# The second half of the row gather and the row scales, moved behind the first down piece

## The chip, the core and the metric

The kernel runs on one core of a Trainium2 chip. The metric is the device time of one execution in microseconds (us); lower is better. Everything is float32 at the inputs and outputs.

## What is computed

A decoder block of 256 tokens with a width of 1024: a token mixer (gated recurrences), a cross-attention, and a mixture of experts, each added to the residual, and a last RMSNorm. The part in question is the mixture:

```
logits = h @ w_router + b_router              # 256 x 32
top_v, top_i = top_k(logits, 4);  gates = softmax(top_v)
for each expert e, for the tokens that chose it:
    gu   = x_rows @ w_gate_up[e] + b_gate_up[e]        # 1024 -> 2048
    gate = min(gu[:, :1024], 7);  up = clip(gu[:, 1024:], -7, 7)
    act  = (up + 1) * gate * sigmoid(1.702 * gate)
    y[tokens] += gates * (act @ w_down[e] + b_down[e]) # 1024 -> 1024
```

There are 32 experts. Each has 8 MiB of gate-and-up weights and 4 MiB of down weights in float32, and about 32 of the 1024 assignments.

## The kernel before, in words

Everything is written out by hand: each engine has one list of instructions in a fixed order, and semaphores are the only thing between the lists.

**Blocks.** Each expert's rows are handled in blocks of 64 (`ROWS`). With the given inputs every expert has one block, so there are 32 blocks; the profile shows it as 32 activations. Expert 0 is the `lead` (it is written out with some extra work), experts 5 to 28 run in a loop of three experts (`LOOPED`), expert 31 is `final` and has an order of its own.

**The weight ring.** The weights go through a ring of 11 slots of 2 MiB (`RING`, `SLOT`). An expert has six pieces: four of gate-and-up (k = 0 to 3) and two of down (k = 4, 5). Experts 0 to 3 and 29 to 31 are loaded piece by piece (L475; L487 for the last expert's down pieces), experts 4 to 28 in pairs of 4 MiB (`load_wide`, L459). All of these transfers are issued by SyncE, in the order of the experts, and each waits until TensorE has used what lay in its slots: `chunk_used` goes up by one at the end of each piece. A pair waits for the use of what lay in the second of its two slots. For instance: the first pair of expert 4 waits for piece (2, 3), its second pair for (2, 5), that is the second down piece of expert 2; its third for (3, 1). Piece (2, 3) waits for (0, 4), the first down piece of expert 0; (3, 3) for (1, 4). Pieces (3, 4), (3, 5) wait for (2, 0), (2, 1).

**One block on TensorE** (`expert`), for an expert that isn't the last:

1. gate-and-up: four pieces, two row tiles each, into `bank_g` and `bank_u` (`pair_of_inner`, L1090; 64 f32 matmul records of 512 columns, two halves of the array side by side). The weights of a piece are waited for (`chunk_in`).
2. `scatter_and_combine`: the rows of the block before are added to the output banks (L1113), and the gate selection is turned over into `bank_d` (L1192).
3. `next_rows(0)`: the first half of the gather for the next block, 24 bf16 matmuls into `bank_a` (L1128). A gather picks the rows of the next block from three bf16 parts of the tokens with the 0/1 matrix `sel`.
4. `flip_act` twice: the activations are turned over, half into `bank_u`, half into `bank_g` (L1201, 4 matmuls). ScalarE copies each half into `actT` (signals `actT_ready` and `actT_rest`).
5. `next_rows(1)`: the second half of the gather, 24 matmuls; then `scales` (L1104, 4 matmuls), which puts the row scales of the next block into `bank_g`, once `actT_rest` says that the bank is free. Its signal is `xb_psum`.
6. down: two pieces, four row tiles each (`pair`, L1081; 16 records per piece). They wait for `comb_ready` and `actT_ready`, and from the third row tile on for `actT_rest`. Each piece signals `chunk_used`.
7. the bias of the next block into `bank_g` and `bank_u` (L1090 again, 4 bf16 matmuls), after `one_hot_ready` and `xb_ready`.

VectorE waits for `xb_psum`, copies the scales (L2262), multiplies the gathered rows by them (L2096, signal `xb_ready`), then makes the selections for the block after the next one (L2072, L2078). ScalarE's activations and copies all have the line of one helper, L1315.

In the last expert the order differs: the two gather halves stand behind the first and second gate-and-up piece, down follows the flip directly, and the scales come after down.

The functions that the change touches:

Of the kernel before, what the change touches and what calls it, by code (L numbers as in the profile page):

```python
# [143 lines left out]
def build(nc, A, out):  # L144

    ctx = ExitStack()
    with ctx:
# [5 lines left out]
        sem = {n: ctx.enter_context(nc.semaphore(n)) for n in SEMS}  # L153
# [14 lines left out]
        def part(slot, first, last):  # L168
            return ring[:, slot * SLOT + first:slot * SLOT + last]
# [465 lines left out]
        def _(pe):  # L635
# [465 lines left out]
            def scales():  # L1101

                for t in range(NT):
                    last = pe.matmul(bank_g[:, 0:ROWS], all_ones, scaled_sel[:, t, :], start=(t == 0), stop=(t == NT - 1))  # L1104
                return last
# [17 lines left out]
            def gather(tiles):  # L1123

                for k in tiles:
                    for i in range(3):
                        for t in range(NT):
                            last = pe.matmul(bank_a[:, k * ROWS:(k + 1) * ROWS], h2_parts[:, i, t, rows_of(k)], sel[:, t, :],  # L1128
                                             start=(i == 0 and t == 0), stop=(i == 2 and t == NT - 1), skip_group_check=True)
                return last  # L1130
# [44 lines left out]
            def expert(e, slots, counts, last_tile=None, lead=False, final=False):  # L1175

                def next_rows(half):
                    pe.wait_ge(sem["sel_ready"], pe.snap(w1 + 1))
                    gather(range(half * KT // 2, (half + 1) * KT // 2))

                def scatter_and_combine():

                    pe.wait_ge(sem["yb_ready"], w1)
                    if lead:
                        pe.wait_ge(sem["down_bias_in"], 32)
                        pe.wait_ge(sem["seeded"], 2 * NT)
                        pe.wait_ge(sem["gT_ready"], 1)
                    scatter()

                    pe.wait_ge(sem["selg_ready"], w1)  # L1190
                    for t in range(NT):
                        last = pe.matmul(bank_d[:, t * P:(t + 1) * P], selg[:, t, :], ident[:, :], start=True, stop=True,  # L1192
                                         is_transpose=True, skip_group_check=True)
                    last.then_inc(sem["comb_psum"], 1)

                def flip_act(bk, half, by_quarter):

                    n = DOWN_ROWS // 2
                    for i in range(n):
                        src = act_t[:, half * QUARTER + i:(half + 1) * QUARTER:n] if by_quarter else act_t[:, half * n + i::DOWN_ROWS]  # L1200
                        last = pe.matmul(bk[:, i * P:(i + 1) * P], src, ident[:, :], start=True, stop=True, is_transpose=True,  # L1201
                                         skip_group_check=True)
                    return last

                if lead:
                    blocks = pe.alloc_register("blocks_of_lead")
                    pe.reg_mov(blocks, 1)
                else:
                    blocks = pe.value_load(table[0:1, bass.ds(e, 1)], min_val=1, max_val=MAXB)
                    first = pe.value_load(table[0:1, bass.ds(e + E, 1)], min_val=0, max_val=MAXW)  # L1210
                with pe.Fori(0, blocks) as c:
                    w1 = pe.snap(c + 1 if lead else first + c + 1)

                    pe.wait_ge(sem["xb_ready"], w1)
                    for k in range(GU_CHUNKS):
                        wk = part(slots[k], 0, SLOT)
                        if counts[k] is not None:
                            pe.wait_ge(chunk_in[slots[k]], counts[k])
                        tiles_of = [(a, bk) for a in range(GU_TILES) for bk in range(2)]
                        if k == GU_CHUNKS - 1 and not final:  # L1220
                            tiles_of = [(a, bk) for bk in range(2) for a in range(GU_TILES)]
                        for a, bk in tiles_of:
                            f = k * GU_TILES + a
                            if lead and (f, bk) == (KT // 2, 0):
                                pe.wait_ge(sem["xb_rest"], 1)
                            if last_tile is not None and (f, bk) == (KT - 1, 0):
                                pe.wait_ge(last_tile, 16)
                            c = a * 2 * D + bk * D
                            last = pair_of_inner((bank_g, bank_u)[bk], xbT[:, f, :], wk[:, c:c + D], False, f == KT - 1)
                            if (f, bk) == (KT - 1, 0):  # L1230
                                last.then_inc(sem["gate_done"], 1)
                            if lead and (f, bk) == (0, 1):
                                last.then_inc(sem["lead_half"], 1)
                        last.then_inc(sem["chunk_used"], 1)
                        if final and k < 2:
                            next_rows(k)
                        if lead and k == 1:
                            pe.wait_ge(sem["table_ready"], 1)
                            pe.reg_load(blocks, table[0:1, 0:1])
                            pe.wait_ge(sem["gates_ready"], 1)  # L1240
                            pe.wait_ge(sem["yb_ready"], w1)
                            one_time()

                    scatter_and_combine()
                    if not final:
                        next_rows(0)

                    pe.wait_ge(sem["act_ready"], w1)
                    if not final:
                        pe.wait_ge(sem["act_rest"], w1)  # L1250
                    flip_act(bank_u, 0, final).then_inc(sem["actT_psum"], 1)
                    if final:
                        pe.wait_ge(sem["act_rest"], w1)
                    flip_act(bank_g, 1, final).then_inc(sem["actT_rest_psum"], 1)

                    if not final:
                        next_rows(1)
                        pe.wait_ge(sem["actT_rest"], w1)
                        pe.wait_ge(sem["scaled_ready"], pe.snap(w1 + 1))
                        scales().then_inc(sem["xb_psum"], 1)  # L1260

                    pe.wait_ge(sem["comb_ready"], w1)
                    pe.wait_ge(sem["actT_ready"], w1)
                    for j in range(DOWN_CHUNKS):
                        wk = part(slots[GU_CHUNKS + j], 0, SLOT)
                        if counts[GU_CHUNKS + j] is not None:
                            pe.wait_ge(chunk_in[slots[GU_CHUNKS + j]], counts[GU_CHUNKS + j])
                        for a in range(DOWN_ROWS):
                            f = DOWN_ROWS * j + a
                            if final:  # L1270
                                h, i = divmod(a, DOWN_ROWS // 2)
                                f = DOWN_ROWS * h + DOWN_ROWS // 2 * j + i
                                if (j, a) == (DOWN_CHUNKS - 1, DOWN_ROWS // 2):
                                    pe.wait_ge(last_half_in, 32)
                                if (j, a) == (DOWN_CHUNKS - 1, 0):
                                    pe.wait_ge(sem["actT_rest"], w1)
                            elif (j, a) == (0, DOWN_ROWS // 2):
                                pe.wait_ge(sem["actT_rest"], w1)
                            last = pair(bank_d, actT[:, f, :], wk[:, a * D:(a + 1) * D], (j, a) == (0, 0),
                                        (j, a) == (DOWN_CHUNKS - 1, DOWN_ROWS - 1))  # L1280
                        last.then_inc(sem["chunk_used"], 1)
                    if final:
                        pe.wait_ge(sem["scaled_ready"], pe.snap(w1 + 1))
                        scales().then_inc(sem["xb_psum"], 1)

                    pe.wait_ge(sem["one_hot_ready"], pe.snap(w1 + 1))
                    pe.wait_ge(sem["xb_ready"], pe.snap(w1 + 1))
                    bias_of(bank_g, 0)
                    bias_of(bank_u, D)
# [1027 lines left out]
```

## Time and profile before

| | |
|---|---|
| median of 3 runs | 1203.46 us (1202.25 to 1204.08) |
| profiled execution | 1201.65 us, its span 1199.9 us |
| mean granted clock of TensorE | 0.986 |
| busy: TensorE | 1149.7 us (96%) |
| busy: VectorE | 378.3 us (32%) |
| busy: ScalarE | 169.7 us (14%) |
| DMA, mean over the span | 371 GB/s |
| read from HBM | 443.20 MB |

The span is the time from the first to the last instruction of the profiled execution. The busy share is an average over stages with different limits; the slices and windows below show them apart. The mixture of experts runs from about 290 us to the end. A matmul's duration in the records includes what it overlaps with its neighbours, so costs on TensorE are better read from the start of one group to the start of the next. `PEld` is the weight load of TensorE, `SPq` the issue of a transfer by SyncE.

### The profile page before, as it was taken

How to read it: one execution, taken by the hardware profiler on the slowest of the kernel's cores; microseconds unless marked ns; L12 is line 12 of the kernel's file. 1: busy time of each engine (PE TensorE's matmuls, PEld its weight loads, DVE VectorE, ACT ScalarE, POOL GpSimd, SP SyncE). 2: the span in 40 equal slices, each digit the busy share in tenths (PEclk: the TensorE clock that was granted, in tenths of full speed). 3: DMA queues.
4: the chain of work that ended last, by engine and by line, in shares of the span. 5: the costliest groups of instructions: out<-in, count | busy, mean ns of one | idle time of the engine just before them, and what ended most of it. 6: DMA issues, size and time to landing. Idle time of an engine off the chain costs nothing.

```text
span 1199.9 us, 17776 instructions
## 1 busy us (share of the span) xinstructions
PE 1149.7 (96%) x7104; PEld 577.8 (48%) x7105; DVE 378.3 (32%) x889; ACT 169.7 (14%) x340; POOL 18.3 (2%) x57
## 2 busy tenths in 40 slices
PE   9999999999999999999999999999999999999996
PEld 5989869956434434333334343333333333333332
DVE  4788777646222221112212121211111111111113
ACT  4311421253100000000001000000000000000002
POOL 2000010000000000000000000000000000000000
PEclk9999999999999999999999999999999999999998
DMA  8953200997999999999999999999999999999995
GB/s 282 387 192 116 107 9 22 399 347 295 413 427 417 430 434 429 430 434 430 433 430 435 429 431 435 428 433 431 435 429 431 433 430 432 434 433 424 424 427 210
DMA packets 41554, 444.85 MB, mean 371 GB/s; under 512 B 6164, under 2 KB 6628, under 8 KB 25640
## 3 DMA queue, kind: packets, MB, share of 16 engines
q1 hardware_dynamic: 40616, 441.62, 88.0%
q0 software_dynamic: 480, 1.85, 0.6%
q10 hardware_dynamic: 416, 0.79, 0.2%
q8 instruction: 29, 0.48, 0.2%
q14 instruction: 13, 0.11, 0.0%
HBM read 443.20 MB, written 1.05 MB: 370 GB/s over the span
## 4 chain that ended last, share of the span: by engine, by line
PE 68%; DMA 31%; ACT 0%; DVE 0%; SPq 0%; issue 0%; DVEq 0%; ACTq 0%
DMA ring<-in_w_gate_up 30%; PE bank L1090 22%; PE bank L1081 13%; PE bank L714 6%; PE bank L710 4%; PE bank L1113 4%; PE bank L1128 3%; PE bank L693 2%; PE bank L702 2%; PE bank L758 2%; PE bank L796 1%; PE bank L1020 1%; PE bank L1201 1%; PE bank L1104 1%; PE bank L1192 1%; PE bank L933 1%
## 5 line engine op out<-in xcount | busy, mean ns | idle before, releaser
L1090 PE MATMUL bank<-ring,region 128*64 128x512 f32 x2048 | 463.8, 608 | 37.5 <-DMA ring<-in_w_gate_up 37.5
L1090 PEld LDWEIGHTS bank<-ring,region 128*64 128x64 f32 x2048 | 147.4, 140 | 335.5 <-issue 270.4
L1081 PE MATMUL bank<-ring,region 128*64 128x512 f32 x1024 | 227.0, 595 | 0.5 <-DMA ring<-in_w_down 0.3
L2116 DVE TENSOR_SCALAR region<-bank 128x512 f32<-128x512 f32 x32 | 22.1, 691 | 575.2 <-PE bank L1090 575.2
L1081 PEld LDWEIGHTS bank<-ring,region 128*64 128x64 f32 x1024 | 71.0, 137 | 130.5 <-issue 126.7
L1315 ACT ACTIVATE region<-bank 128x256 f32<-128x256 f32 (+1 forms) x134 | 55.5, 440 | 372.7 <-PE bank L1081 251.5
L1315 ACT ACTIVATE bank<-region 128x512 f32<-128x512 f32 x32 | 19.2, 602 | 453.8 <-DVE region L2116 453.8
L714 PE MATMUL bank<-ring 128*128 128x256 f32 x336 | 73.8, 380 | 0.0
L714 PEld LDWEIGHTS bank<-ring 128*128 128x128 f32 x336 | 63.3, 190 | 9.3 <-issue 0.5
L1113 PE MATMUL bank<-region 64*128 64x512 f32 x264 | 65.6, 615 | 0.0
L1128 PEld LDWEIGHTS bank<-region,r_levels 128*128 128x128 bf16 x1584 | 63.1, 117 | 1.8 <-issue 1.6
L1128 PE MATMUL bank<-region,r_levels 128*128 128x64 bf16 x1584 | 63.3, 197 | 0.0
L710 PE MATMUL bank<-ring 128*128 128x128 f32 x448 | 50.7, 275 | 0.0
L710 PEld LDWEIGHTS bank<-ring 128*128 128x128 f32 x448 | 50.3, 192 | 0.3 <-issue 0.2
L1113 PEld LDWEIGHTS bank<-region 64*128 64x128 f32 x264 | 22.7, 186 | 41.9 <-issue 41.5
L1315 ACT ACTIVATE ring<-bank 128x256 f32<-128x256 f32 (+4 forms) x64 | 26.3, 433 | 116.6 <-PE bank L714 45.4
L2119 DVE TENSOR_SCALAR region<-bank 128x512 f32<-128x512 f32 x32 | 22.1, 691 | 32.0 <-PE bank L1090 32.0
L2262 DVE COPY stat<-bank 128x64 f32<-128x64 f32 x31 | 7.0, 225 | 58.5 <-PE bank L1104 58.5
L2072 DVE TENSOR_SCALAR region<-region 128x64 bf16 (+1 forms) x64 | 13.3, 251 | 37.8 <-issue 37.8
L1201 PE MATMUL bank<-ident,region 128*128 128x128 f32 x128 | 23.2, 304 | 0.0
L2123 DVE SCALAR_TENSOR_TENSOR region<-region 128x512 f32<-128x512 f32 x32 | 22.2, 692 | 3.3
L2096 DVE TENSOR_TENSOR region<-bank,stat 128x512 f32<-128x512 f32 (+1 forms) x33 | 22.3, 674 | 1.7 <-PE bank L1128 0.6
(279 smaller groups left out, 783.1 us busy)
## 6 DMA issues: line engine op xcount, KB each, us to landing
ring<-in_w_gate_up SPq DMA_DIRECT2D x50, 4096.0 KB, 29.8
ring<-in_w_down SPq DMA_DIRECT2D x25, 4096.0 KB, 34.4
ring<-in_w_gate_up SPq DMA_DIRECT2D x24, 2048.0 KB, 16.6
ring<-in_w_down SPq DMA_DIRECT2D x11, 2048.0 KB, 11.7
ring<-in_w_in SPq DMA_DIRECT2D x6, 2048.0 KB, 17.8
ring<-in_w_xkv SPq DMA_DIRECT2D x4, 2048.0 KB, 10.2
ring<-in_w_gate_up SPq DMA_DIRECT2D x7, 1024.0 KB, 35.2
ring<-in_w_out SPq DMA_DIRECT2D x2, 2048.0 KB, 8.0
```

What stands on the lines that cost most here:

```text
L693: last = pe.matmul(bk[:, i * T:(i + 1) * T], w[:, k, (m + i) * P:(m + i + 1) * P], rhs[:, k, :], start=(k == 0), stop=(k == KT - 1))
L702: last = pe.matmul(bk[:, :], lhs[:, k, t * P:(t + 1) * P], w[:, k, :], start=(k == 0), stop=(k == KT - 1))
L710: last = pe.matmul(bk[:, i * P:(i + 1) * P], right[:, k, i * P:(i + 1) * P], left[:, k, :], start=(first and i == 0 and k == 0), stop=(k = ...
L714: last = pe.matmul(bk[:, 0:T], left[:, k, :], right[:, k, :], start=(first and k == 0), stop=(k == 3), skip_group_check=True)
L758: last = pe.matmul(bk[p:p + m, c * m:(c + 1) * m], rows[:, j * P + p:j * P + p + m], rows[:, i * P + p + shift:i * P + p + shift + m], sta ...
L1081: last = pe.matmul(bk[half * ROWS:(half + 1) * ROWS, :], lhs, w[:, half * 512:(half + 1) * 512], start=start, stop=stop, skip_group_check= ...
L1090: last = pe.matmul(rows, lhs, columns[:, half], start=start, stop=stop, skip_group_check=True)
L1113: last = pe.matmul(bank_y[t][half][:, :], combT[rows, t * P:(t + 1) * P], yb[rows, :], start=False, stop=False, skip_group_check=True)
L1128: last = pe.matmul(bank_a[:, k * ROWS:(k + 1) * ROWS], h2_parts[:, i, t, rows_of(k)], sel[:, t, :], start=(i == 0 and t == 0), stop=(i == ...
L1201: last = pe.matmul(bk[:, i * P:(i + 1) * P], src, ident[:, :], start=True, stop=True, is_transpose=True, skip_group_check=True)
L1315: return nc.scalar.activation(out_, in_, func, **kw)
L2096: v.tensor_tensor(xbT[:, lo:hi, :], src, row_scales.unsqueeze(1).broadcast_to([P, hi - lo, ROWS]), ALU.mult).then_inc(signal, 1)
```

## The change

The block of `next_rows(1)`, the wait for `scaled_ready` and `scales()` is taken from between the flip and the down stage, and put behind the first of the two down pieces. Its wait for `actT_rest` is dropped; the down loop has the same wait ahead of the third row tile of the first piece, so it has been passed by then. The last expert isn't changed.

```diff
@@ -1253,12 +1253,6 @@
                         pe.wait_ge(sem["act_rest"], w1)
                     flip_act(bank_g, 1, final).then_inc(sem["actT_rest_psum"], 1)
 
-                    if not final:
-                        next_rows(1)
-                        pe.wait_ge(sem["actT_rest"], w1)
-                        pe.wait_ge(sem["scaled_ready"], pe.snap(w1 + 1))
-                        scales().then_inc(sem["xb_psum"], 1)
-
                     pe.wait_ge(sem["comb_ready"], w1)
                     pe.wait_ge(sem["actT_ready"], w1)
                     for j in range(DOWN_CHUNKS):
@@ -1279,6 +1273,10 @@
                             last = pair(bank_d, actT[:, f, :], wk[:, a * D:(a + 1) * D], (j, a) == (0, 0),
                                         (j, a) == (DOWN_CHUNKS - 1, DOWN_ROWS - 1))
                         last.then_inc(sem["chunk_used"], 1)
+                        if j == 0 and not final:
+                            next_rows(1)
+                            pe.wait_ge(sem["scaled_ready"], pe.snap(w1 + 1))
+                            scales().then_inc(sem["xb_psum"], 1)
                     if final:
                         pe.wait_ge(sem["scaled_ready"], pe.snap(w1 + 1))
                         scales().then_inc(sem["xb_psum"], 1)
```

## Rows read from the trace of the kernel before

**Rows 1.** The page, part 2: GB/s of the DMA in 40 equal slices.
```profile
GB/s 282 387 192 116 107 9 22 399 347 295 413 427 417 430 434 429 430 434 430 433 430 435 429 431 435 428 433 431 435 429 431 433 430 432 434 433 424 424 427 210
```
**Rows 2.** Windows by stage: us, busy of each engine, granted clock, DMA share, GB/s.
```profile
370.00:376.00 6.00, 6.00 (x32) 2.10 (x30) 0.00 (x0) 0.60 (x1) 0.00 (x0) 1.00 0.96 374
...
450.00:550.00 100.00, 100.00 (x646) 41.15 (x644) 20.38 (x52) 8.98 (x20) 0.00 (x0) 1.00 1.00 430
600.00:700.00 100.00, 93.62 (x592) 37.54 (x591) 18.27 (x50) 8.21 (x19) 0.00 (x0) 0.97 1.00 432
```
**Rows 3.** Waits of TensorE over the span: us in total, times, longest.
```profile
PE bank L1090 <- DMA ring<-in_w_gate_up: 37.5, 23, 2.6
```
**Rows 4.** Chain of waits, 330 to 375: start, us, what; down of experts 1 and 2.
```profile
339.33 7.02 PE bank L1081 x32
...
365.45 7.02 PE bank L1081 x32
```
**Rows 5.** Timeline at 1170 to 1178: start, us, engine, line, tiles, idle before.
```profile
1175.47 0.39 PEld L1090 LDWEIGHTS bank<-ring,region 128*64 128x64 f32 x4 [0.47 <-DMA ring<-in_w_gate_up]
```
**Rows 6.** Timeline at 362 to 373: the turn of expert 2.
```profile
363.45 0.73 PE L1201 MATMUL bank<-ident,region 128*128 128x128 f32 x4
...
363.97 0.66 ACT L1315 ACTIVATE region<-bank 128x256 f32<-128x256 f32 x2 [0.74 <-PE bank L1201]
364.02 0.96 PE L1128 MATMUL bank<-region,r_levels 128*128 128x64 bf16 x24
...
364.81 0.64 PE L1104 MATMUL bank<-scaled_sel,region 128*128 128x64 f32 x4
...
365.38 7.09 PE L1081 MATMUL bank<-ring,region 128*64 128x512 f32 x32
...
365.75 0.69 DVE L2096 TENSOR_TENSOR region<-bank,stat 128x512 f32<-128x512 f32 x1
365.86 0.14 PEld L1081 LDWEIGHTS bank<-ring,region 128*64 128x64 f32 x2 [0.28 <-issue]
...
372.30 0.62 PE L1090 MATMUL bank<-region 128*64 128x512 bf16 x4
...
372.51 0.33 SPq L459 DMA_DIRECT2D ring<-in_w_gate_up  x1
```
**Rows 7.** Timeline at 1126 to 1200: expert 30's down, the last expert's gather and down.
```profile
1156.11 3.65 PE L1081 MATMUL bank<-ring,region 128*64 128x512 f32 x16 [0.27 <-DMA ring<-in_w_down]
1159.59 0.62 PE L1090 MATMUL bank<-region 128*64 128x512 bf16 x4
...
1160.83 3.65 PE L1090 MATMUL bank<-ring,region 128*64 128x512 f32 x16 [0.61 <-DMA ring<-in_w_gate_up]
1164.41 0.88 PEld L1128 LDWEIGHTS bank<-region,r_levels 128*128 128x128 bf16 x24 [0.81 <-issue]
...
1179.73 0.76 PE L1201 MATMUL bank<-ident,region 128*128 128x128 f32 x4
...
1180.68 7.09 PE L1081 MATMUL bank<-ring,region 128*64 128x512 f32 x32 [0.20 <-ACT region L1315]
```
**Rows 8.** Transfers issued around 245, 316, 360 and at 372.5 (landing alone), by line.
```profile
L475 SPq DMA_DIRECT2D ring<-in_w_gate_up x2: 327/385/443, 245.5 to 245.9; - x2
...
DMA to landing us min/median/max: 8.0/9.6/11.2
...
L475 SPq DMA_DIRECT2D ring<-in_w_gate_up x1: 340/340/340, 316.8 to 316.8; - x1
...
DMA to landing us min/median/max: 9.2/9.2/9.2
...
L459 SPq DMA_DIRECT2D ring<-in_w_gate_up x1: 328/328/328, 360.6 to 360.6; - x1
...
DMA to landing us min/median/max: 14.4/14.4/14.4
...
DMA to landing us min/median/max: 12.4/12.4/12.4
```

## The prediction

> **What bounds the kernel now.** I read the page first: busy shares, then the DMA line of the 40 slices. TensorE is busy 96% of the span, and from the eleventh slice on, up to the last, the DMA moves 413 to 435 GB/s [rows 1]. Both look full, so the page alone can't say which one ends the time. The windows by stage can [rows 2]: TensorE is busy 100 of 100 us at 450 to 550, but 93.6 at 600 to 700, while the DMA share is 1.00 in both, at 430 and 432 GB/s. The waits say the same: TensorE waited 37.5 us in all, 23 times, and for gate-and-up weights [rows 3].
>
> The reason is in two prices. An expert's weights are six pieces of 2 MiB, 12.58 MB, at 431 GB/s 29.2 us. An expert costs TensorE 26.12 us, from one down stage to the next, 339.33 to 365.45 [rows 4]. TensorE is the faster of the two by 3.1 us per expert. At first it eats the stock of loaded pieces and never waits; somewhere between 550 and 700 the stock is gone, and from there it follows the transfers. The end too hangs on a transfer: the last gate-and-up tile releases TensorE at 1175.47 [rows 5], and the 24.4 us behind it are the last expert and the output, which the change doesn't touch. So the time is the start of the weight stream, plus its bytes at 431 GB/s, plus any gap in it, plus 24.4 us. The question about any edit in the expert loop is whether it opens or closes a gap in the stream.
>
> **What the block costs TensorE.** I read the turn of expert 2, which repeats in all 31 experts that aren't the last, and take starts of one group to starts of the next [rows 6]. The flip of the activations (L1201) starts at 363.45, the second half of the gather (L1128, 24 matmuls) at 364.02, the scales (L1104, 4 matmuls) at 364.81, the down stage (L1081, 32 records) at 365.38, the bias behind it (L1090) at 372.30. That is 0.57, 0.79, 0.57 and 6.92 us, 8.85 in all, with no idle time ahead of any of them.
>
> The gather and the scales are moved, not removed: 0.79 and 0.57 are paid again behind the first down piece. Two things are new.
>
> 1. The cover of ScalarE's copies is gone. Down can't start until ScalarE has copied the first flipped half out of the bank (actT_ready). Its two copies start at 363.97 and take 0.66 together [rows 6]; the gather lay over them. The last expert already has no gather there and shows the naked path: flip at 1179.73, down at 1180.68, "idle before, ScalarE" [rows 7]. That is 0.95 against 0.57: +0.38 us. Bounds: a first copy done after half of the 0.66 gives 364.30, +0.28 over 364.02; waiting for both (364.63, and 0.09 more for the handover) gives +0.70. I take 0.38, the row of the same path. The second copy (actT_rest) is wanted two row tiles into the piece, 1.7 us later, and is hidden.
> 2. Down is cut in two. The same shape of run, 16 records and then a gather, stands in the last expert: 1160.83 to 1164.41, 3.58 us; and 16 down records and then the bias, 1156.11 to 1159.59, 3.48 us [rows 7]. Together 7.06 against 6.92 unsplit: +0.14. Bounds: 0, and 0.53, if the weight loads' pause of 0.81 ahead of that gather [rows 7] counted in full over the usual 0.28 [rows 6].
>
> So TensorE pays 0.52 us more per block (bounds 0.28 to 1.23).
>
> What else hangs on the step: VectorE copies the scales and scales the gathered rows behind the scales matmuls, and the bias waits for that (xb_ready). Now this is done at 365.75 + 0.69 = 366.44, 1.06 us after down's start, with 5.9 us to spare [rows 6]. After the change it is done 1.06 us into the second piece, which lasts 3.48: 2.4 us to spare, cost 0; if that cover were gone the excess would be paid in each block. VectorE's selections for the block after next follow that multiply and come 4.0 us later (0.95 + 3.58 + 0.79 + 0.57 = 5.89 after the flip against 1.93); they are wanted by a gather some 20 us on. Queued behind TensorE's new wait for actT_ready are only its own down matmuls. SyncE's queue gets no new instruction, but it waits for pieces used: the first down piece is now used 0.95 + 3.58 = 4.53 us after the flip instead of 1.93 + 3.46 = 5.39, so 0.86 us earlier; the second one 0.52 later. The wide transfers (expert 4 to 28) all wait for the second piece of a pair, so the earlier signal helps only single-piece transfers.
>
> **What of it reaches the stream.** 0.52 us on TensorE costs nothing where the DMA queue has work: 26.1 + 0.5 = 26.6 is still under 29.2, and in the waiting stage the waits shrink by as much. It costs only where a transfer is issued into an empty queue. I went through the issues one by one. A 4 MiB transfer at 431 GB/s takes 9.7 us.
> - Issued at 360.57, landed 14.4 later at 375.0 [rows 8]: 4.7 us of it was queue.
> - Issued at 372.51, landed 12.4 later at 384.9 [rows 8]: 9.9 behind its predecessor, against 9.7 for the bytes. This one found the queue empty: 12.4 - 9.7 = 2.7 us is the naked start-up, and 372.51 + 2.7 = 375.2 is just behind 375.0. A 2 MiB transfer issued at 245.5 into an empty queue took 8.0 for 4.9 of bytes, so 3.1 [rows 8]. The window 370 to 376 moves only 374 GB/s [rows 2]: (431 - 374) x 6 / 431 = 0.8 us are lost already.
> - From there the queue gets deeper by the 3.1 us per expert that TensorE is ahead, which is why 450 to 550 has a full share [rows 2].
>
> The transfer at 372.51 is the second pair of expert 4. It waits for the last down piece of expert 2: the issue stands 0.21 us behind the start of the bias [rows 6]. By then three changed blocks have passed (experts 0, 1, 2), so it is issued 3 x 0.52 = 1.56 us later, at 374.07, and lands at 386.5. Everything behind it moves by that, since the queue isn't empty again. The transfers before it have room: the one at 360.57 has 4.7 - 2.7 = 2.0 us, and is late by two blocks, 1.04. The single pieces that wait for a first down piece (one of them issued at 316.8, landed 9.2 later, 4.3 of it queue [rows 8]) gain 0.86 less earlier shifts, and had queue ahead of them: no gain.
>
> At the tail, expert 30's second down piece waited 0.27 us for its weights, and the tile after it 0.61 [rows 7]. The new order gets to the second piece 5.89 - 1.93 - 3.46 = 0.50 later; 0.27 of that goes into the one wait and 0.23 into the other, and the last expert starts as before.
>
> The sum: against the profiled execution's own 1201.65 us (span 1199.9 and 1.75 around it) +1.56, which I round to 1.5 since single DMA engines may still have had a little queue: 1203.2. The profiled run lies 1.8 below the median of the three; on the median of 1203.46 it is 1205.0. Bounds 3 x 0.28 = 0.8 and 3 x 1.23 = 3.7.
>
> The Trainium skill, "DMA: Bandwidth & Descriptors", in its cost components, puts the fixed part of a transfer at about 2.0 us where these rows have 2.7 and 3.1. By it the transfer at 372.51 would still have had 375.0 - 374.5 = 0.5 us of room, and the change would cost an estimated 1.1 us instead of 1.5. The measurements here decide for the larger.
>
> **The rivals.**
> - *Slower by more than 2.4 us.* The one mechanism is the same starved transfer, with a dearer block: ScalarE's copies and the cut array cost TensorE over 0.8 us. 3 x 0.8 = 2.4 is the point from which it decides; at the upper bounds it is 3.7, 1207.2. For it: both prices are read from the last expert only, where ScalarE's order of copies is another. Against: the upper bounds need both copies waited for, which the code doesn't ask. 0.16.
> - *TensorE is the bound after all.* 31 x 0.52 = 16 us, 1219.6. Only if the stream weren't full; the shares of 1.00 speak against it. 0.02.
> - *Hidden altogether.* The late issue finds each of the 16 DMA engines still busy, or the restart in step recovers what a lagging engine lost. Then 1203.5. For it: landing times are those of the slowest engine. Against: the lost 0.8 us in that window. 0.18.
> - *Faster.* The first down piece is released 0.86 us earlier, and if one of the early single-piece transfers is what sets the stream's phase, the whole stream moves up by that: 1202.6. Against: all of them had over 4 us of queue. 0.10.
> - *That it doesn't do what it says:* the order on TensorE's queue is the program's, so I give it nothing.
>
> **The numbers.** My case, +0.5 to +2.4, has 0.54. A measurement of this kernel tells about 0.2% from no change, 2.4 us. My own case, the hidden one and most of the faster one lie within it; beyond it on the slow side lie the dear block, the bound TensorE and a little of my own case's upper edge, 0.22; on the fast side what is left of the third and what I haven't thought of, 0.08. The time is 1205.0; the range 1202.5 to 1207.2 takes in the faster case at its low end and the bounds of the block's price at its high one.
>
> **What would show it.** The down records in two groups of 16 with 24 gathers and 4 scales between; an idle of about 0.2 to 0.4 us before down, put down to ScalarE; from flip to bias 9.37 us instead of 8.85; an expert of 26.6 us before 550; the first wide transfers issued at 361.6 and 374.1, the second still landing 12.4 later; TensorE's waits for weights 8 to 15 us smaller than 37.5; the last gate-and-up tile 1.5 us later; no wait of the bias for VectorE. If the second wide transfer is late by 1.5 and the last tile isn't, the step from the gap to the end is wrong. If TensorE's block costs over 0.8 us or nothing, its price is.

## The result

| | median, us | runs | ratio, 95% interval |
|---|---|---|---|
| before | 1202.97 (1201.41 to 1204.56) | 12 | |
| after | 1204.74 (1203.67 to 1206.48) | 12 | 1.0018 (1.001 to 1.0026) |

The change costs 1.8 us by the medians, 2.2 by the ratio (1.2 to 3.1). I had forecast +1.5 on the three runs shown. The profiled execution of after has a span of 1202.9 us against 1199.9. That pair of executions shows 3.0, more than the medians, and 0.4 of it was there before the first expert began. Executions of one and the same kernel, before included, scatter by some 2 us, and in the profiled ones part of that stands ahead of the experts (the first weight transfer past 230 us is issued at 231.6 to 232.2 us in eleven traces and at 233.9 to 234.0 in those of e1, e4 and e8), so a difference of under 1 us between two medians says little.

### The profile page after: what moved, and what is told of

Read it like the earlier page. It is cut to its first block, busy times and chain, and to the rows that moved or that the text cites. A ratio compares the mean times of both kernels' runs of the same rounds, so it can differ in the third digit from the quotient of the medians.

```text
span 1202.9 us, 17745 instructions
## 1 busy us (share of the span) xinstructions
PE 1158.9 (96%) x7104; PEld 582.1 (48%) x7105; DVE 378.6 (31%) x889; ACT 169.8 (14%) x340; POOL 18.5 (2%) x57
## 4 chain that ended last, share of the span: by engine, by line
PE 72%; DMA 26%; issue 1%; ACT 0%; DVE 0%; SPq 0%; DVEq 0%; ACTq 0%
DMA ring<-in_w_gate_up 26%; PE bank L1090 24%; PE bank L1081 14%; PE bank L714 6%; PE bank L710 4%; PE bank L1113 4%; PE bank L1128 3%; PE bank L693 2%; PE bank L702 2%; PE bank L758 2%; PE bank L796 1%; PE bank L1020 1%; PE bank L1201 1%; PE bank L1104 1%; PE bank L1192 1%
## 5 line engine op out<-in xcount | busy, mean ns | idle before, releaser
L1090 PEld LDWEIGHTS bank<-ring,region 128*64 128x64 f32 x2048 | 148.6, 140 | 316.8 <-issue 272.9
L1081 PEld LDWEIGHTS bank<-ring,region 128*64 128x64 f32 x1024 | 73.3, 136 | 122.9 <-issue 120.5
L1313 ACT ACTIVATE region<-bank 128x256 f32<-128x256 f32 (+1 forms) x134 | 55.5, 439 | 393.0 <-PE bank L1081 271.5
L1313 ACT ACTIVATE bank<-region 128x512 f32<-128x512 f32 x32 | 19.2, 602 | 436.4 <-DVE region L2114 436.4
L1128 PEld LDWEIGHTS bank<-region,r_levels 128*128 128x128 bf16 x1584 | 60.5, 118 | 26.9 <-issue 26.8
L1313 ACT ACTIVATE ring<-bank 128x256 f32<-128x256 f32 (+4 forms) x64 | 26.3, 433 | 116.6 <-PE bank L714 45.4
```

Source lines behind the costliest of these rows:

```text
L1081: last = pe.matmul(bk[half * ROWS:(half + 1) * ROWS, :], lhs, w[:, half * 512:(half + 1) * 512], start=start, stop=stop, skip_group_check= ...
L1090: last = pe.matmul(rows, lhs, columns[:, half], start=start, stop=stop, skip_group_check=True)
L1313: return nc.scalar.activation(out_, in_, func, **kw)
```

## The profile after

The turn of expert 2 in the timeline of after (start, us, engine, line, tiles, idle before). The line numbers of VectorE and ScalarE are smaller by two than before; L1313 is L1315 of before. It answers to [rows 6].

```profile
365.10 0.73 PE L1201 MATMUL bank<-ident,region 128*128 128x128 f32 x4
365.63 0.66 ACT L1313 ACTIVATE region<-bank 128x256 f32<-128x256 f32 x2 [0.73 <-PE bank L1201]
...
366.11 3.65 PE L1081 MATMUL bank<-ring,region 128*64 128x512 f32 x16 [0.28 <-issue]
...
369.70 0.98 PE L1128 MATMUL bank<-region,r_levels 128*128 128x64 bf16 x24
...
370.52 0.64 PE L1104 MATMUL bank<-scaled_sel,region 128*128 128x64 f32 x4
...
371.08 3.65 PE L1081 MATMUL bank<-ring,region 128*64 128x512 f32 x16
...
371.45 0.69 DVE L2094 TENSOR_TENSOR region<-bank,stat 128x512 f32<-128x512 f32 x1
...
374.57 0.62 PE L1090 MATMUL bank<-region 128*64 128x512 bf16 x4
...
374.78 0.33 SPq L459 DMA_DIRECT2D ring<-in_w_gate_up  x1
```

From start to start: flip 1.01, first piece 3.59, gather 0.82, scales 0.56, second piece 3.49, together 9.47 us, where it was 8.85 [rows 6]. A block costs 0.62 us more: 0.44 between flip and down (the first activation copy's cover), 0.16 for the cut, 0.02 in the moved part. I take the 0.28 of idle ahead of down as the wait for ScalarE's copy: it isn't there before, and it is gone in e7, where the gather lies over the copy again. The profile books this pause as "issue" in 24 places and to ScalarE in 8. One of the 24 is the last expert's 0.20, which was there before. These are TensorE's waits over the whole span of after (us in total, times, longest), which answer to [rows 3]:

```profile
PE bank L1090 <- DMA ring<-in_w_gate_up: 22.4, 16, 2.2
PE bank L1081 <- issue: 6.6, 24, 0.3
PE bank L1081 <- ACT region L1313: 3.3, 8, 0.4
```

The waits for weights fell by 15.1 us, from 37.5. That is where most of 31 x 0.62 = 19 us went: TensorE was ahead of the weights and now is less so. The transfers issued by SyncE at 362.2 and 374.8, with their time to landing (each pair of lines is one window of the view by line):

```profile
L459 SPq DMA_DIRECT2D ring<-in_w_gate_up x1: 328/328/328, 362.2 to 362.2; - x1
...
DMA to landing us min/median/max: 13.6/13.6/13.6
...
L459 SPq DMA_DIRECT2D ring<-in_w_gate_up x1: 328/328/328, 374.8 to 374.8; - x1
...
DMA to landing us min/median/max: 12.6/12.6/12.6
```

The second pair of expert 4 is issued 2.27 us later than before (0.37 of that is the later start of the experts) and lands 12.6 us behind its issue, so 11.5 behind its predecessor (387.37 against 375.86), where the bytes need 9.7. The gap grew from 0.3 to 1.8 us. By windows (us, busy of each engine, granted clock, DMA share, GB/s), against [rows 2]:

```profile
450.00:550.00 100.00, 99.02 (x614) 39.68 (x616) 18.87 (x50) 7.93 (x17) 0.00 (x0) 1.00 1.00 429
370.00:376.00 6.00, 6.00 (x51) 2.85 (x50) 1.78 (x6) 0.60 (x1) 0.00 (x0) 1.00 0.84 330
480.00:510.00 30.00, 29.72 (x186) 11.98 (x184) 6.18 (x18) 2.84 (x6) 0.00 (x0) 1.00 0.99 419
600.00:700.00 100.00, 96.08 (x608) 38.91 (x606) 20.74 (x54) 8.38 (x19) 0.00 (x0) 0.98 1.01 433
```

370 to 376 fell from 374 to 330 GB/s. There is a second dent that I hadn't forecast, 419 at 480 to 510 where the kernel before moved 430. This is the line of before:

```profile
480.00:510.00 30.00, 30.00 (x186) 11.98 (x184) 5.31 (x14) 2.25 (x5) 0.00 (x0) 1.00 1.00 430
```

The tail is different too. The waits of TensorE from 1090 us to the end of after:

```profile
PE bank L1090 <- DMA ring<-in_w_gate_up: 2.0, 1, 2.0
PE bank L1081 <- issue: 1.0, 4, 0.3
```

The last wait for weights is at 1089.45. The last gate-and-up tile, whose wait [rows 5] shows, is waited for no longer.

## The experiments

Theory 1: the delay of experts 0 to 2 reaches one transfer that is issued into an empty queue, and the stream carries it to the end. Theory 2: it is paid in the tail. Rival 3: TensorE is the bound, so each block pays. A dose is extra work on TensorE alone: the gather of a block repeated, which writes the same values again. Times are against runs of the kernel before on the same chip (medians 1202.11 for e1 to e4, 1202.57 for e5 to e8, 1202.15 for e9 to e12); the last column is what the ratio is above 1, times 1202 us.

| run | change against before | median, us | ratio, 95% interval | us |
|---|---|---|---|---|
| e1_head_moved | new order in experts 0-4 | 1205.13 | 1.0016 (1.0007 to 1.0025) | +1.9 |
| e2_rest_moved | new order in 5-30 | 1203.24 | 1.0006 (0.9998 to 1.0015) | +0.7 |
| e3_head_dose | 4.8 us of gathers in 0-2 | 1206.21 | 1.0040 (1.0027 to 1.0053) | +4.8 |
| e4_loop_dose | 38 us of gathers in 5-28 | 1203.02 | 1.0004 (0.9995 to 1.0013) | +0.5 |
| e5_single4_old | expert 4 in single pieces | 1201.52 | 0.9991 (0.9982 to 1.0) | -1.1 |
| e6_single4_new | the same, with the new order | 1203.49 | 1.0007 (0.9998 to 1.0016) | +0.8 |
| e7_scales_only | only the scales moved | 1203.35 | 1.0003 (0.9994 to 1.0012) | +0.4 |
| e8_expert3_dose | 5.95 us in expert 3 | 1205.12 | 1.0023 (1.0014 to 1.0032) | +2.8 |
| e9_dose_expert2 | 2.4 us in expert 2 | 1204.08 | 1.0015 (1.0006 to 1.0024) | +1.8 |
| e10_dose_expert3 | 2.4 us in expert 3 | 1202.46 | 1.0002 (0.9993 to 1.0011) | +0.2 |
| e11_tail_dose | 3.2 us in 29 and 30 | 1203.12 | 1.0007 (0.9998 to 1.0016) | +0.8 |
| e12_dose_single4 | dose of e3, loads of e5 | 1204.17 | 1.0019 (1.001 to 1.0028) | +2.3 |

### Where the new order costs: e1 and e2

```diff
-                    if not final:
+                    if not final and not moved:
                         next_rows(1)
...
+                        if j == 0 and moved and not final:
+                            next_rows(1)
```
with `moved` true for experts 0 to 4 (e1) or for the others (e2).

> The new order in experts 0 to 4 only, the old one in the others. A changed block costs TensorE 0.62 us in the trace after the change. Theory 1, gap in the weight stream: the second pair of expert 4 waits for expert 2 and is issued 3 x 0.62 = 1.9 us later into an empty queue, all behind it moves: +1.9 us, the same as the whole change. Theory 2, the last experts: the trace after the change shows no wait for weights behind 1090 us, so the changed blocks there are what is paid: here +0. Rival 3, TensorE is the bound everywhere: 5 x 0.62 = +3.1.

> The new order in experts 5 to 30, the old one in 0 to 4. Theory 1: the second pair of expert 4 is issued as before; the next transfer with little queue ahead, the first pair of expert 8 (issued at 477 with 6.5 us of queue, 2.7 of which are start-up), is 2 x 0.62 = 1.2 later and has 3.8 to spare: +0 to +0.3. Theory 2: up to 3 x 0.62 = 1.9 us in experts 28 to 30, less the 4.4 us of waits that stand there in the kernel before: +0 to +1.9. Rival 3: 26 x 0.62 = +16.

Five changed blocks of 31 give the whole cost, +1.9 (0.8 to 3.0). The other 26 give +0.7 (-0.2 to 1.8), which isn't clear of zero, and the two intervals overlap; the table of the traces below tells them apart better. Rival 3 (+16 for e2) is out. Theory 2 isn't needed for the 1.8, but e2 leaves room for a part in it.

### What TensorE's time is worth, by place: e3, e4, e8, e9, e10

```diff
                     if not final:
-                        next_rows(1)
+                        for _ in range(1 + extra):
+                            next_rows(1)
```
`extra` is 2 in experts 0 to 2 (e3), 2 in the loop (e4), 6 in expert 3 (e8), 3 in expert 2 (e9), 3 in expert 3 (e10).

> The kernel before, with the second half of the gather done three times instead of once in experts 0, 1 and 2 (the repeats write the same values): 2 x 0.79 us more TensorE per block, 4.7 in all before the second pair of expert 4 can be issued. Theory 1: the late issue passes one to one, +4.7 us, the transfer still lands 12.4 after its issue. If single DMA engines had work left, less: +3 to +4.5. Theory 2: +0, since nothing is changed in the last experts.

> The kernel before, with the same two repeats of the gather in each of the 24 experts of the loop (5 to 28): 38 us more TensorE work, 26.1 + 1.6 = 27.7 us per expert against 29.2 us of weights. Theory 1: the work goes into waits for weights; the first pair of expert 8 comes 3.2 later with 3.8 to spare: +0 to +1 us. Theory 2: +0 to +1.6 from expert 28. Rival 3: +38.

> The kernel before, with the second half of the gather done seven times in expert 3 alone: 6 x 0.79 = 4.7 us, the same dose that experts 0 to 2 got together in e3_head_dose, one expert later. Theory 1: the transfers that wait for expert 3's down (second pair of expert 5, issued at 398.6 with 7.2 us of queue, 2.7 of them start-up) have 4.5 us to spare: +0 to +0.5 us, against the +4 of the same dose before the starved transfer. If any delay of TensorE in the early experts counted, +4 again.

> The kernel before, with the second half of the gather done four times in expert 2 alone. Each repeat costs 0.80 us of TensorE in the trace of e3_head_dose: +2.4 us, just ahead of the starved transfer (second pair of expert 4). Theory 1: it passes one to one, +2.4 us.

> The kernel before, with the same dose of 2.4 us in expert 3 alone. In e8_expert3_dose the dose was in truth 5.95 us (4.8 of matmuls and 1.15 of fetching), over the 4.5 that the second pair of expert 5 has to spare. 2.4 is under it, and under the 3.8 of the first pair of expert 8. Theory 1: +0 to +0.5 us, against +2.4 one expert earlier. If early delay counted wherever it is: +2.4.

4.8 us in the experts ahead of the starved transfer cost 4.8 (3.2 to 6.4); 38 us in the 24 experts of the loop cost 0.5 (-0.6 to 1.6). e8 missed. Its chain of waits (start, us, what) says why:

```profile
392.64 5.59 PE bank L1128 x168
398.23 0.47 PE bank L1104 x4
398.71 1.15 issue
399.86 2.33 PE bank L1081 x9
```

The seven gathers took 5.59 us, 4.79 more than one, and behind them TensorE stood for another 1.15 in "issue", waiting for nothing that the profile shows. The dose was 5.95 us, over the 4.5 to spare, and the second pair of expert 5 starved in its turn (that alone would cost 1.5, and the run shows 2.8; more on this at the table of the traces):

```profile
L459 SPq DMA_DIRECT2D ring<-in_w_gate_up x1: 328/328/328, 407.0 to 407.0; - x1
...
DMA to landing us min/median/max: 12.0/12.0/12.0
```

12.0 us for 4 MiB is a naked transfer again; in the kernel before the same one had 7.2 us of queue ahead when it was issued. So I repeated the test with 2.4 us in one expert: +1.8 in expert 2, +0.2 in expert 3, one expert later. The windows 370 to 376 of these two, e9 first, then e10:

```profile
370.00:376.00 6.00, 6.00 (x32) 2.10 (x30) 0.86 (x4) 0.60 (x1) 0.00 (x0) 1.00 0.52 221
```
```profile
370.00:376.00 6.00, 6.00 (x32) 2.10 (x30) 0.00 (x0) 0.60 (x1) 0.00 (x0) 1.00 0.97 380
```

The gap opens in the one (221 GB/s) and is that of the kernel before in the other (380 against 374). The intervals of the two just overlap (1.0006 to 1.0024, 0.9993 to 1.0011); e3 against e4 is the clear pair.

The traces say where the stream loses its time, with less scatter than the times. The table counts the bytes that the DMA view of each trace gives from the first weight transfer issued past 230 us on (231.72 in before), over stretches of 118, 158, 230 and 900 us. These end ahead of the starved transfer, behind it, ahead of the second dent, and near the end. A kernel that has moved 0.431 MB less than before is 1 us late. The last four columns give this delay in us, good to about 0.4 (in 900 us before moved 380.03 MB, after 378.93). The column "issue" is that of the second pair of expert 4, in us from the same start.

| trace | issue | 118 | 158 | 230 | 900 |
|---|---|---|---|---|---|
| before | 140.8 | 0 | 0 | 0 | 0 |
| after | 142.7 | -0.3 | 1.7 | 1.9 | 2.6 |
| e1 (new order in 0-4) | 142.7 | -0.1 | 1.6 | 1.9 | 1.9 |
| e2 (new order in 5-30) | 140.8 | 0.4 | 0.4 | 0.4 | 0.4 |
| e3 (4.8 us in 0-2) | 145.6 | 1.0 | 4.8 | 4.8 | 4.8 |
| e4 (38 us in 5-28) | 140.8 | -0.3 | 0.3 | 0.3 | 1.3 |
| e7 (scales only) | 141.6 | 0.1 | 1.0 | 1.2 | 1.1 |
| e8 (5.95 us in 3) | 140.8 | -0.4 | 0.2 | 2.9 | 3.4 |
| e9 (2.4 us in 2) | 143.2 | 0.3 | 2.5 | 2.3 | 2.4 |
| e10 (2.4 us in 3) | 140.8 | 0.2 | 0.1 | 1.0 | 0.9 |
| e11 (3.2 us in 29, 30) | 140.8 | 0.1 | 0.0 | -0.1 | 0.0 |
| e5 (single pieces) | - | 0.2 | -0.5 | -0.6 | -0.6 |
| e6 (single pieces, new order) | - | -0.4 | -0.7 | -0.2 | 1.6 |
| e12 (single pieces, 4.8 us in 0-2) | - | 1.2 | 1.7 | 2.1 | 2.5 |

Where nothing was changed ahead of it the transfer is issued at 140.8 in all six traces, and the stream has lost 0.4 or less at 158. In after, e1, e9 and e3 it is issued 1.9, 1.9, 2.4 and 4.8 later, and the stream has lost 1.7, 1.6, 2.5 and 4.8. From 158 to 900 e1, e3 and e9 change by 0.3 at most. So the late issue is carried to the end, as theory 1 has it. In e3, 1.0 of the 4.8 was already lost at 118, at single pieces ahead of this transfer. e10 is less clean than its time: in its trace the stream lost 0.9 between 158 and 230, although the second pair of expert 5, issued at 400.9, still had 4.6 us of queue, 1.9 over the start-up. And e8 lost 2.9 there, so the 4.5 us to spare were nearer 3.

### Taking the starved transfer away: e5, e6, e12

```diff
-HALVED = 4
+HALVED = 5
```

> The kernel before (old order), with expert 4 loaded in six single pieces instead of three pairs (HALVED = 5). Its third piece then waits for the first down piece of expert 2 instead of the second one, so it is issued at 369 instead of 372.5, while the queue still has work until 375. Theory 1: the gap behind 372 closes; what it costs the kernel before is the 0.8 us that the window 370 to 376 lacks: -0.3 to -0.9 us. Rival: single pieces use the DMA engines less well than pairs, +0 to +0.5.

> The kernel after the change (new order in all blocks), with expert 4 loaded in single pieces. Theory 1: its third piece waits for a first down piece, issued at about 370 with the queue busy until 376, so the starved transfer is gone, and with it nearly the whole cost of the change: within 0.5 us of the kernel before, and 0 to 1 us above the same loads with the old order. Theory 2 or a price in each block: the 1.8 us stay.

> Expert 4 in single pieces (as e5_single4_old, which took 1.0 us less than before), with the dose of e3_head_dose: 4.8 us more TensorE in experts 0 to 2, which cost +4.1 to +4.8 with pairs. Theory 1: the starved transfer is gone, the next tight one is the second pair of expert 5 (6.1 us of queue, 2.7 of start-up, 3.4 to spare): 4.8 - 3.4 = 1.4 us over e5, and up to 1.5 more for DMA engines that run ahead of the slowest: +0.4 to +2 against the kernel before. If the dose counted by itself: +3.8 against before.

With single pieces the old order gains 1.1 us and the window 370 to 376 is full. This is the fastest of all versions, at the edge of what the runs can tell from before. But e6 missed: the new order still costs 0.8 against before and some 1.9 against e5. Windows of e5, then of e6:

```profile
370.00:376.00 6.00, 6.00 (x32) 2.10 (x30) 0.00 (x0) 0.60 (x1) 0.00 (x0) 1.00 1.02 431
480.00:510.00 30.00, 30.00 (x188) 11.99 (x185) 5.32 (x14) 2.25 (x5) 0.00 (x0) 1.00 1.00 430
```
```profile
370.00:376.00 6.00, 6.00 (x49) 2.83 (x48) 1.78 (x6) 0.60 (x1) 0.00 (x0) 1.00 0.99 423
480.00:510.00 30.00, 29.72 (x186) 11.93 (x184) 6.18 (x18) 2.84 (x6) 0.00 (x0) 1.00 0.95 398
```

The first gap is closed in e6, and the loss sits in a later tight place: (430 - 398) x 30 / 430 = 2.2 us at 480 to 510 (1.8 in the table of the traces, from -0.2 to 1.6). There the first pair of expert 8 waits for the second down piece of expert 6, behind seven changed blocks. The stream that isn't held up at 372 runs further ahead of TensorE (by 2.1 us at 230, e6 against after), so TensorE's delay of 7 x 0.62 = 4.3 us bites there instead. Delay isn't added over the places: a gap at one place gives room at the next. e12 halves the price of e3's dose, 2.3 instead of 4.8 against before. It was above the range that I had written by 0.3, and not for the reason that I had written: the second pair of expert 5 was to be the tight place, but in the trace 1.2 us were lost by 118 us and 1.7 by 158, at the single pieces, and only 0.4 between 158 and 230.

### The two prices apart, and the tail: e7, e11

In e7 only `scales()` and its wait stand in the `if j == 0` block, and `next_rows(1)` stays; e11 has `extra` 2 in experts 29 and 30.

> Only the scales are moved behind the first down piece; the gather half stays in front of down. It takes the two new prices apart: ScalarE's copy is covered by the gather again, the down stage is still cut in two. Measured together they are 0.62 us per block. I expect 0.15 to 0.25 us per block, so 3 times that for the time: +0.5 to +0.8 us, against +1.8 if the cut were the whole price.

> The kernel before, with two repeats of the gather half in experts 29 and 30: 3.2 us more of TensorE in the tail, where the trace of before has 3.2 us of waits for weights behind 1110 us. Theory 2 in its strong form (TensorE sets the tail): +3.2 us. My forecast's step (swallowed by the waits): +0 to +1 us. The changed order puts 1.2 us there.

The chain of waits of e7 through experts 1 and 2:

```profile
339.00 3.58 PE bank L1081 x16
342.59 0.59 PE bank L1104 x4
343.18 3.58 PE bank L1081 x16
...
365.39 3.58 PE bank L1081 x16
```

An expert takes 26.39 us there, 26.12 before [rows 4], 26.74 after (339.37 to 366.11 for the first down piece). By this split the cut is 0.27 of the 0.62 and the uncovered copy 0.35. The time agrees in size (+0.4, three blocks of 0.27 are 0.8) but isn't told from zero. e11: 3.2 us in the tail cost 0.8, so some three quarters are swallowed, as forecast; the interval takes in both 0 and 1.9. Its stream is that of before (0.0 at 900 in the table of the traces).

## Why the prediction was right

- *The number.* Forecast +1.5 and 1205.0, measured +1.8 (2.2 by the ratio) and 1204.74. That the time itself is met within 0.3 us is luck: the change cost more than forecast, and the median of before, 1203.46 in three runs, is 0.5 lower in twelve. The sum had one term. By the traces that term was 1.9, and two others, which the sum had at nothing, were not: the stream lost 0.7 more at the second dent, and TensorE 0.7 in the tail (both below).
- *The bound.* Right. The weight stream sets the time, and 38 us of TensorE work in the loop change it by 0.5 (e4). One line was misread: the wait that ends at 1175.47 [rows 5] is that of a weight load. The matmuls don't wait for weights from 1170.52 on, so 29.4 us and not 24.4 stand behind that last wait.
- *The price of a block.* Forecast 0.52, measured 0.62, inside the bounds 0.28 to 1.23. The term that was too small is the uncovered copy: 0.44 from flip to down, not the 0.38 read from the last expert, where ScalarE began its copies 0.20 us behind the start of the flip (1179.93) instead of 0.53 (365.63). The cut was 0.16 by start-to-start (forecast 0.14); e7, with another order of the pieces, puts 0.27 on it.
- *The covers.* Right. The gathered rows are ready at 371.45 + 0.69 = 372.14, 2.4 us ahead of the bias at 374.57, as worked out, and no wait of the bias shows.
- *The starved transfer.* Right, and shown by place: e1, e3 and e9 against e4 and e10. The step from the late issue to the end, one to one, was 4.8 (3.2 to 6.4) for 4.8 in e3, 1.8 (0.7 to 2.9) for 2.4 in e9, and in their traces 4.8 and 2.4.
- *"The queue isn't empty again."* Here the prediction was wrong. I followed the queue only up to expert 5 and took the growth of 3.1 us per expert for granted. The first pair of expert 8 waits for expert 6's last piece and is issued late, at 481.9 with 3.7 us of queue ahead (the transfer before it landed at 485.6), 1.0 over the start-up where the kernel before had 3.8:

```profile
L459 SPq DMA_DIRECT2D ring<-in_w_gate_up x1: 328/328/328, 481.9 to 481.9; - x1
...
DMA to landing us min/median/max: 13.7/13.7/13.7
...
L459 SPq DMA_DIRECT2D ring<-in_w_gate_up x1: 328/328/328, 489.2 to 489.2; - x1
...
DMA to landing us min/median/max: 17.3/17.3/17.3
```

  They land at 495.6 and 506.5, 10.9 apart where the bytes need 9.7, and the window there lacks (430 - 419) x 30 / 430 = 0.8 us. So the queue wasn't empty by the landings, and the stream still lost some 0.7 us. In after it is small, because the gap behind 374 had already held the stream back; in e6 it is the main loss.
- *The tail.* Half right. I had the last experts swallow their 0.5 us, and they nearly do (e11). But the waits there ran out, and in this execution TensorE goes through from 1089.45 to the end without one for weights. Its own part can be read off at the third gate-and-up piece of the last expert. In before the last wait for weights that holds TensorE up ends there; in after the piece lands at 1172.8, and TensorE is 0.7 us behind it. First before, then the piece and TensorE in after:

```profile
1170.52 7.09 PE L1090 MATMUL bank<-ring,region 128*64 128x512 f32 x32 [0.32 <-DMA ring<-in_w_gate_up]
```
```profile
L475 SPq DMA_DIRECT2D ring<-in_w_gate_up x1: 328/328/328, 1132.6 to 1132.6; - x1
...
DMA to landing us min/median/max: 40.2/40.2/40.2
```
```profile
1173.50 7.09 PE L1090 MATMUL bank<-ring,region 128*64 128x512 f32 x32
```

  So of the 3.0 us between the two profiled spans 0.4 is the later start, 0.7 the tail, and 1.9 the stream, whose piece landed 2.3 later with the 0.4 in it (the last piece too, where the forecast had 1.5). By bytes the stream was 2.6 late; in before one down piece of expert 30 landed at 1156.1, 6.7 us behind its predecessor for 4.9 us of bytes, and from there on the landings of the two traces are that much closer. In e11 TensorE is 1.1 us behind that piece, in e2, with the same tail as after, it still waits for it. How much of the median's 1.8 comes from the tail the runs can't tell from nothing.
- *The other cases.* The first pieces of down were released earlier and gave nothing. The dear block would have needed 0.8 us.
- *The signs.* TensorE's waits for weights fell by 15.1 us, at the edge of the 8 to 15 forecast, and the idle ahead of down was booked as "issue" and not to ScalarE in most places.

The starved transfers took 12.4 us (before), 12.6 (after), 12.2 (e3) and 12.0 (e8) for 9.7 us of bytes, so the fixed part was 2.3 to 2.9 us. The Trainium skill, "DMA: Bandwidth & Descriptors", in its cost components, has about 2.0, from a fit to transfers that GpSimd issues; these are SyncE's, and the measurements are above it. The room of 0.5 us that it would have left at 372.5 isn't seen in the traces of e1 and e3, where 1.9 and 4.8 us of delay became 1.9 and 4.8 us of stream; the times alone can't tell 0.5.

## What to carry to other kernels

Where a stream of transfers is the bound, ask of an edit on the compute engine not how much it costs but which transfer is issued late by it, and how much queue that one has ahead of it, less the start-up of a transfer. List this room for every issue of the stream up to the point where the compute engine waits, since a closed gap can move the loss to a later tight place. And count on less room than the landings give: transfers with 1.0 (after), 1.9 (e10) and 2.6 us (e4, issued at 482.4, its predecessor landed at 487.7) left by this rule went with losses of 0.7, 0.9 and 1.0 us. And before work is moved from between a producer's matmuls and their consumer, look what copy it was covering.

## What the runs showed of the hardware

- 38 us of extra matmuls, 1.6 in each of 24 experts, cost 0.5 us: with them TensorE is busy 100 of 100 us at 600 to 700 and the DMA still moves 433 GB/s.
- 168 gather matmuls in a row (e8) were followed by 1.15 us in which TensorE waited for nothing that the profile shows; 96 in a row (e9) weren't: from 364.35 to 368.01 its chain has only the gathers and the scales. Nor were those in e10, with the same 96. The expectation of e10 calls the 1.15 fetching. The trace of e8 has a 16 KB packet of the instruction queue at 397.3, but other traces have such packets without a pause beside them, so that cause isn't shown.
- A transfer may land some 1.5 us behind its turn although it had queue ahead: in before 405.8 behind 394.6 for 9.7 us of bytes, with 7.9 us of queue; in e5 464.6 behind 453.4, with 14.4 us of queue and no starved transfer before it.
- The second pair of expert 4, issued at 140.8 in six traces with nothing changed ahead of it, landed 12.4 (before), 13.7, 14.1, 14.3, 14.3 and 14.4 us later. One landing is a poor measure of the stream; the issue and the bytes moved are better. The view gives one landing for a transfer and not one for each DMA engine, so what lags isn't seen.
